# Expert results weighted as they leave PSUM and added to the residual rows in DRAM by an accumulating scatter

## The chip, the cores and the metric

One core of one Trainium2 chip runs the kernel. The metric is the device time of one execution in microseconds (us), lower is better. The timed runs of a kernel carry no profile; one more run is profiled, and every duration of the rows below comes from that one.

## What is computed

A transformer block with two halves. The first half (a hybrid mixer of spatial gating, chunked linear attention and a short convolution) gives the rows `x2 = x + gt1 * mixer`. The second half is a mixture of experts over the 1024 rows: 32 experts in 4 groups, each token goes to the best 2 experts of one group. Then one RMS norm over the sum.

```python
def moe(h, router_w, router_b, w1, w3, w2):
    ...
    weights = top_p / jnp.sum(top_p, axis=-1, keepdims=True)
    ...
    def expert_block(args):
        xb, e = args
        return (jax.nn.silu(xb @ w1[e]) * (xb @ w3[e])) @ w2[e]
    ...
    out = jnp.einsum('nk,nkd->nd', weights.astype(h.dtype), y_assign)
...
        x = x + gt2 * moe(h, router_w, router_b, exp_w1[l], exp_w3[l], exp_w2[l])
    return rmsnorm(x, g_final)
```

T = 1024 rows of D = 1024 float32 values, 512 hidden values in an expert; an expert has three matrices (w1, w3, w2) of 2 MiB each, so 32 experts are 96 units of 2 MiB.

## The kernel before

The program is written by hand for each engine, with semaphores between them; an engine's instructions run in the order of the code. The 1024 rows are 8 tiles of 128. The first 500 us are the mixer. Between about 440 and 530 us the rows x2 are made tile by tile and stored in the DRAM tensor `x2_dram` (a normed copy goes to `xn2_dram`), and the router runs for two tiles at a time: `choose` picks the two experts of each token, `weigh` (from L1685) makes its two shares `top_w`, `place` its position in each expert's list. The matmuls of `listing` (L976) build the lists of rows for each expert, and after the experts have been ranked by their number of rows three small matmuls (L1021 to L1023) give `slot_i`: for each of 25 passes and each of 128 partitions the assignment (2 x token + choice) that the partition holds, or a number past the end where it holds none. `slot_tok` is half of it, the token.

**The expert loop** has 25 passes. Passes 0 to 3 are single: one expert, up to 128 rows. Then come 7 triples of a couple pass (two experts with up to 64 rows each, in the two halves of the partitions) and two single passes; a couple uses 6 units of weights, a single 3. In pass i:

- SP loads the units in the order of `stream` into 9 slots; the load of a unit waits until the unit 9 places before it has been used (`load_unit`, L506).
- POOL gathers the rows of pass i+4 from `xn2_dram` (`gather`, L667) and scatters the result of pass i-1 (`scatter`, L675).
- PE turns the gathered rows (L1030), multiplies by w1 and w3 (L1044 for a single, L1049 for a couple), turns the hidden rows (L1057) and multiplies by w2 (L1068 or L1074) into banks 5 and 6.
- DVE takes the result out of the banks times the gate gt2 (`y_evac`, L1806) into one of two buffers `y_sb`; it may overwrite a buffer when the scatter of two passes before has landed.

The scatter of before writes each row of `y_sb` to row `slot_i` of `y_dram`, which has one row for each assignment (2048 rows). No two writes touch the same row, so scatters may overlap in time; rows without an assignment are past the bound and are dropped.

**The tail.** SP waits for all scatters, then loads `y_dram` (8 MiB) in five pieces of 1, 1, 2, 2 and 2 tiles into `yy` (L567). The residual rows `acc` were loaded before that (L547), once their two slots were free. For each tile DVE adds the first choice times its share (L1894) and the second (L1898); ACT sums the squares (L1327); DVE makes the mean (L1339); POOL raises it to the power -0.5 (L586, where the shared `rsqrt` stands); DVE applies it and the gain (L1888); ACT issues the store of the tile (L1323). A branch for experts whose lists are too long (`most > 0`) follows the loop; it isn't entered with these inputs.

## Time and profile before

| | us |
|---|---|
| median of 3 timed runs | 1165.42 |
| their range | 1164.93 to 1166.04 |
| the profiled execution | 1166.22 |
| its span, first to last instruction | 1164.5 |

The span is shorter than the execution by 1.7 us, which lie around it. The rows of the profile name source lines: L1044 is line 1044 of the kernel before. Busy times of matmul are close to the wall time where PE is the bound. "Landing" of a DMA counts from its issue to the last write. The chain that ended last follows the waits back from the end of the program.

### The profile page before, as it was taken

To read this page: it belongs to the slowest core of one execution; us is meant where nothing else is said; L and a number is where in the kernel's file an instruction comes from. 1 tells how busy PE (TensorE), PEld (TensorE's weight loads), DVE (VectorE), ACT (ScalarE), POOL (GpSimd) and SP (SyncE) were. 2 spreads that over 40 slices of the span, in tenths; PEclk is the share of its full clock that TensorE was granted. 3 is DMA by queue.
4 is the path that set the end of the run, shared out by engine and by line. 5 is a ranking of instruction groups with operands and counts; after the bars stand their busy time and mean duration, and the time that the engine had idled before them with its cause. 6 is when DMAs were issued, how large, how long until landed. Compare 5 with 4: busy or idle time off the path is not lost.

```text
span 1164.5 us, 11977 instructions
## 1 busy us (share of the span) xinstructions
PE 1047.4 (90%) x4616; PEld 611.4 (53%) x4616; DVE 394.7 (34%) x827; ACT 198.7 (17%) x435; POOL 106.8 (9%) x135
## 2 busy tenths in 40 slices
PE   4798999999999999943999999999999999999920
PEld 2487888878896555532444443444444344444410
DVE  2588543426631355551111211211111121121137
ACT  5611125222221121110100100100010010010002
POOL 2000000002100010123010010001001001000013
PEclk9899999999999999955999999999999999999975
DMA  9829311112132662137688999999999999997446
GB/s 370 305 73 343 130 37 37 39 53 91 37 127 91 235 252 92 55 127 261 244 308 329 391 422 387 426 397 405 399 405 416 372 427 385 408 375 302 165 199 243
DMA packets 52555, 295.76 MB, mean 254 GB/s; under 512 B 11129, under 2 KB 23434, under 8 KB 36114
## 3 DMA queue, kind: packets, MB, share of 16 engines
q1 hardware_dynamic: 43634, 274.00, 60.3%
q0 software_dynamic: 7712, 16.80, 3.7%
q10 hardware_dynamic: 1152, 4.19, 0.9%
q8 instruction: 37, 0.61, 0.2%
q14 instruction: 20, 0.16, 0.0%
HBM read 278.55 MB, written 25.85 MB: 261 GB/s over the span
## 4 chain that ended last, share of the span: by engine, by line
PE 87%; DMA 5%; DVE 3%; issue 1%; DVEq 1%; ACT 1%; POOL 1%; SPq 0%; ACTq 0%; POOLq 0%
PE bank L1044 22%; PE bank L1068 11%; PE bank L937 10%; PE bank L1049 8%; PE bank L1074 4%; PE bank L778 3%; PE bank L773 3%; PE bank L775 3%; PE bank L774 3%; PE bank L779 3%; PE bank L780 3%; PE bank L1030 2%; DMA arena<-in_x_dram 1%; PE bank L732 1%; PE bank L955 1%
## 5 line engine op out<-in xcount | busy, mean ns | idle before, releaser
L1044 PE MATMUL bank<-arena 128*128 128x512 f32 x576 | 255.9, 600 | 1.6 <-ACT arena L1295 1.6
L1044 PEld LDWEIGHTS bank<-arena 128*128 128x128 f32 x576 | 109.2, 192 | 145.3 <-issue 143.3
L1068 PE MATMUL bank<-arena 128*128 128x512 f32 x288 | 127.9, 597 | 1.7 <-issue 1.7
L937 PE MATMUL bank<-arena 128*128 128x512 f32 x256 | 114.6, 602 | 0.1
L1049 PE MATMUL bank<-arena 128*64 128x512 f32 x448 | 99.2, 595 | 0.0
L1303 ACT ACTIVATE arena<-bank 128x512 f32<-128x512 f32 x25 | 14.9, 597 | 470.1 <-PE bank L1044 334.2
L778 PE MATMUL bank<-low_r 128*128 128x256 f32 (+1 forms) x320 | 93.7, 293 | 0.0
L779 PE MATMUL bank<-low_r 128*128 128x256 f32 (+1 forms) x320 | 90.8, 284 | 0.0
L780 PE MATMUL bank<-low_r 128*128 128x256 f32 (+1 forms) x320 | 90.8, 284 | 0.0
L1068 PEld LDWEIGHTS bank<-arena 128*128 128x128 f32 x288 | 53.2, 190 | 63.8 <-issue 62.3
L773 PE MATMUL bank<-low_r 128*128 128x512 f32 x192 | 78.1, 407 | 4.9 <-DVE arena L1448 3.7
L1806 DVE TENSOR_TENSOR arena<-bank,arena 128x512 f32<-128x512 f32 x50 | 32.2, 686 | 145.9 <-PE bank L1068 105.3
L937 PEld LDWEIGHTS bank<-arena 128*128 128x128 f32 x256 | 48.1, 192 | 55.8 <-issue 55.8
L774 PE MATMUL bank<-low_r 128*128 128x512 f32 x192 | 76.1, 396 | 0.0
L775 PE MATMUL bank<-low_r 128*128 128x512 f32 x192 | 76.0, 396 | 0.0
L586 POOL TENSOR_TENSOR stats<-stats,half 128x1 f32<-128x1 f32 (+1 forms) x34 | 31.1, 918 | 482.2 <-DVE stats L1339 455.4
L1800 DVE COPY arena<-bank 128x512 f32<-128x512 f32 x25 | 17.3, 692 | 164.2 <-PE bank L1057 164.2
L675 POOL DMA_INDIRECT y_dram<-arena,slot_i x25 | 25.1, 1004 | 506.0 <-DVE arena L1806 506.0
L1049 PEld LDWEIGHTS bank<-arena 128*64 128x64 f32 x448 | 30.9, 137 | 66.6 <-issue 66.6
L1822 DVE TENSOR_TENSOR arena<-bank,arena 128x512 f32<-128x512 f32 x25 | 17.3, 692 | 141.9 <-PE bank L1044 101.7
L778 PEld LDWEIGHTS bank<-low_r 128*128 128x128 f32 x320 | 60.9, 190 | 3.4 <-issue 2.7
L779 PEld LDWEIGHTS bank<-low_r 128*128 128x128 f32 x320 | 61.0, 191 | 0.0
(246 smaller groups left out, 1131.0 us busy)
## 6 DMA issues: line engine op xcount, KB each, us to landing
arena<-in_exp_w_dram SPq DMA_DIRECT2D x96, 2048.0 KB, 11.2
arena<-in_w_ada_dram SPq DMA_DIRECT2D x24, 1024.0 KB, 9.1
low<-in_w_in_dram SPq DMA_DIRECT2D x11, 1024.0 KB, 5.5
arena<-y_dram SPq DMA_DIRECT2D x3, 2048.0 KB, 17.1
arena<-in_x_dram SPq DMA_DIRECT2D x2, 2048.0 KB, 7.8
arena<-in_w_out_dram SPq DMA_DIRECT2D x2, 2048.0 KB, 8.7
arena<-in_x_dram SPq DMA_DIRECT2D x8, 512.0 KB, 3.6
x_dram<-arena SPq DMA_DIRECT2D x8, 512.0 KB, 2.6
```

The costliest lines, as they stand in the source:

```text
L773: pe.matmul(out_[:], hi[:, k, f_], hT_hi[:, k, t_], start=first, stop=False)
L774: pe.matmul(out_[:], lo[:, k, f_], hT_hi[:, k, t_], start=False, stop=False)
L775: mm = pe.matmul(out_[:], hi[:, k, f_], hT_lo[:, k, t_], start=False, stop=last)
L778: pe.matmul(w, hT_hi[:, k, t_], hi[:, k, :], start=first, stop=False)
L779: pe.matmul(w, hT_hi[:, k, t_], lo[:, k, :], start=False, stop=False)
L780: mm = pe.matmul(w, hT_lo[:, k, t_], hi[:, k, :], start=False, stop=last)
L937: mm = pe.matmul(bank[2 * (t % 2) + n][:], yT[:, t, k, :], wout[n][:, k, :], start=(k == 0), stop=(k == KD - 1))
L1044: mm = pe.matmul(out_[:], x[:, k, :], ws[0][:, k, :], start=(k == 0), stop=(k == KD - 1))
L1049: mm = pe.matmul(out_[rows_, :], x[:, k, rows_], w[:, k, :], start=(k == 0), stop=(k == KD - 1))
L1068: mm = pe.matmul(bank[5 + j][:], hT_sb[:, k, :], ws[0][:, k, cols], start=(k == 0), stop=(k == KF - 1))
L1074: mm = pe.matmul(bank[5 + j][rows_, :], hT_sb[:, k, rows_], w[:, k, cols], start=(k == 0), stop=(k == KF - 1))
L1806: ins = TT(y_sb[i % 2][:, j * 512:(j + 1) * 512], bank[5 + j][:], gt2[:, j * 512:(j + 1) * 512], ALU.mult)
```

## The change

- `y_dram` is gone. The rows are scattered into `x2_dram` itself, indexed by the token, with `compute_op=ALU.add`: the DMA reads the old row, adds, and writes.
- The share of each row is applied earlier: `y_evac` multiplies bank, the share `slot_w` of the partition and gt2 in one scalar_tensor_tensor. To have the share by partition, the lists carry a second set of 32 columns: `weigh` writes `named` also with top_w (one drain and two multiplications more), the matmul of `listing` has 64 columns of `named` where it had 32, and three more matmuls pick the shares, after three more DVE instructions (`fits`, `fits`, `share_f`) ahead of `list_f`.
- Every scatter waits until the one before has landed (`scat` is one semaphore now). A couple pass, in which a token may stand twice, is scattered as two transfers of 128 rows, each with the other half's rows past the bound (`half_tok`). That makes 32 scatters of 25.
- In the tail `acc` is loaded after the last scatter, in the same five pieces, at 4 MiB in all, and the early load of 4 MiB is gone. The 16 multiply-adds of L1894 and L1898 are gone; ACT waits for the pieces itself.

The diff, without the branch that isn't entered:

```diff
     xn2_dram = nc.dram_tensor("xn2_dram", (T, D), F32, kind="Internal").ap()
-    y_dram = nc.dram_tensor("y_dram", (2 * T, D), F32, kind="Internal").ap()
+    share_dram = nc.dram_tensor("share_dram", (2 * T, 1), F32, kind="Internal").ap()
     gate_dram = nc.dram_tensor("gate_dram", (2, D), F32, kind="Internal").ap()
...
-        sel, named, r_["t"] = (X.take(4, E) for _ in range(3))
+        sel, named, r_["t"] = X.take(4, E), X.take(4, 2 * E), X.take(4, E)
         M = Region(TMP_AT, TMP_END)
...
         y_sb = [M.take(D) for _ in range(2)]
-        list_f = y_sb[0][0:E, P:2 * P]
+        list_f, share_f = y_sb[0][0:E, P:2 * P], y_sb[0][0:E, 2 * P:3 * P]
+        fits = y_sb[0][0:E, 0:1]
+        slot_w, ov_share = M.take(PASSES), M.take(1)
+        half_tok = M.take(2, COUPLES).bitcast(I32)
         key_row, above = y_sb[1][0:E, 0:E], y_sb[1][0:E, E:2 * E]
...
                          .rearrange("p a n -> p (a n)")).then_inc(S["early_ld"], 16)
-            for s in acc_slots:
-                kind, i, _ = [u for n, u in enumerate(stream) if n % SLOTS == s][-1]
-                sp.wait_ge(S[{"w1": "h1_mm", "w2": "y_mm", "w3": "h3_mm"}[kind]], i + 1)
-            sp.dma_start(acc, x2_dram.rearrange("(t p) d -> p t d", p=P)).then_inc(S["early_ld"], 16)
-
             most = sp.value_load(most_i[0:1, 0:1], min_val=0, max_val=T)
...
-            for h in range(2):
-                sp.wait_ge(scat[h], 16 * ((PASSES + 1 - h) // 2))
+            sp.wait_ge(scat, 16 * added[-1])
             for h, (a, b) in enumerate(y_parts):
-                sp.dma_start(yy[:, a:b, :], y_t[:, a:b, :]).then_inc(y_ld[h], 16)
+                sp.dma_start(acc[:, a:b, :], x2_p[:, a:b, :]).then_inc(y_ld[h], 16)
             sp.wait_ge(out_st, 16 * TILES)
...
                 gp.wait_ge(S["y_ready"], i + 1)
-                gp.sem_inc(S["gp_passed"], 1)
-                gp.indirect_dma_start(out=y_dram, out_offset=bass.IndirectOffsetOnAxis(ap=slot_i[:, c_:c_ + 1], axis=0),
-                                      in_=y_sb[i % 2], in_offset=None, bounds_check=2 * T - 1,
-                                      oob_is_err=False).then_inc(scat[i % 2], 16)
+                for n in range(len(passes[i])):
+                    tok = slot_tok[:, c_:c_ + 1] if len(passes[i]) == 1 else half_tok[:, n, c_ - WIDE:c_ - WIDE + 1]
+                    wait(gp, scat, 16 * (added[i] - len(passes[i]) + n))
+                    gp.sem_inc(S["gp_passed"], 1)
+                    gp.indirect_dma_start(out=x2_dram, out_offset=bass.IndirectOffsetOnAxis(ap=tok, axis=0),
+                                          in_=y_sb[i % 2], in_offset=None, bounds_check=T - 1,
+                                          oob_is_err=False, compute_op=ALU.add).then_inc(scat, 16)
...
                 for n in range(4):
-                    mm = pe.matmul(bank[7][0:E, P:2 * P], named[:, n, :], placed[:, n, :], start=(i == 0 and n == 0),
+                    mm = pe.matmul(bank[7][0:2 * E, P:2 * P], named[:, n, :], placed[:, n, :], start=(i == 0 and n == 0),
                                    stop=(i == TILES // 2 - 1 and n == 3), skip_group_check=True)
...
             pe.wait_ge(S["list_ready"], 1)
-            pe.matmul(bank[7][:, 0:WIDE], list_f, ranked[:, 0:WIDE], start=True, stop=True)
-            pe.matmul(bank[7][0:HALF, WIDE:PASSES], list_f[:, 0:HALF], ranked[:, WIDE:WIDE + COUPLES], start=True, stop=True)
-            pe.matmul(bank[7][HALF:P, WIDE:PASSES], list_f[:, 0:HALF], ranked[:, WIDE + COUPLES:E], start=True,
-                      stop=True).then_inc(S["slots_mm"], 1)
+            for at_, lists in ((0, list_f), (PASSES, share_f)):
+                wide_, couple_ = slice(at_, at_ + WIDE), slice(at_ + WIDE, at_ + PASSES)
+                pe.matmul(bank[7][:, wide_], lists, ranked[:, 0:WIDE], start=True, stop=True)
+                pe.matmul(bank[7][0:HALF, couple_], lists[:, 0:HALF], ranked[:, WIDE:WIDE + COUPLES], start=True, stop=True)
+                mm = pe.matmul(bank[7][HALF:P, couple_], lists[:, 0:HALF], ranked[:, WIDE + COUPLES:E], start=True, stop=True)
+            mm.then_inc(S["slots_mm"], 1)
...
             for t in range(TILES):
-                act.wait_ge(S["fin_acc"], t + 1)
+                for h, (a, b) in enumerate(y_parts):
+                    if a == t:
+                        act.wait_ge(y_ld[h], y_ld_was[h] + 16)
                 act.activation(sq_junk, acc[:, t, :], ACT.Square, accum_out=ssf[:, t:t + 1])
...
                     dve.tensor_reduce(top2[:, :, k], by_tile2(g_["r" if k else "t"]), AX, ALU.add)
-                    TT(named[:, 2 * k:2 * k + 2, :], sel[:, 2 * k:2 * k + 2, :], each(aid_f[:, ts, k], E), ALU.mult)
+                    TT(named[:, 2 * k:2 * k + 2, 0:E], sel[:, 2 * k:2 * k + 2, :], each(aid_f[:, ts, k], E), ALU.mult)
                     TT(r_["t"][:, 2 * k:2 * k + 2, :], sel[:, 2 * k:2 * k + 2, :], eidx.unsqueeze(1).to_broadcast([P, 2, E]), ALU.mult)
...
                 TT(top_w[:, ts, :], top2, each(w_rec, 2), ALU.mult)
+                dve.drain()
+                for k in range(2):
+                    TT(named[:, 2 * k:2 * k + 2, E:], sel[:, 2 * k:2 * k + 2, :], each(top_w[:, ts, k], E), ALU.mult)
...
             dve.wait_ge(S["list_mm"], TILES // 2)
+
+            TS(fits, sort_col[:, 4:5], float(WIDE), float(cap - HALF), ALU.is_lt, ALU.mult)
+            dve.drain()
+            STT(fits, fits, float(HALF), sort_col[:, 2:3], ALU.add, ALU.is_ge)
+            dve.drain()
+            TS(share_f, bank[7][E:2 * E, P:2 * P], fits, None, ALU.mult)
             TS(list_f, bank[7][0:E, P:2 * P], float(NONE), None, ALU.add).then_inc(S["list_ready"], 1)
...
             TS(slot_tok, slot_i, 1, None, ALU.logical_shift_right).then_inc(S["slots_ready"], 1)
+            dve.memset(half_tok.rearrange("p a b -> p (a b)"), 2 * T)
+            dve.drain()
+            for n in range(2):
+                rows_ = slice(n * HALF, (n + 1) * HALF)
+                dve.tensor_copy(half_tok[rows_, n, :], slot_tok[rows_, WIDE:PASSES])
+            dve.tensor_copy(slot_w, bank[7][:, PASSES:2 * PASSES])
+            dve.drain()
...
                 dve.wait_ge(S["y_mm"], i + 1)
-                wait(dve, scat[i % 2], 16 * (i // 2))
+                if i >= 2:
+                    dve.wait_ge(scat, 16 * added[i - 2])
+                c_ = passes[i][0]
                 for j in range(2):
-                    ins = TT(y_sb[i % 2][:, j * 512:(j + 1) * 512], bank[5 + j][:],
-                             gt2[:, j * 512:(j + 1) * 512], ALU.mult)
+                    ins = STT(y_sb[i % 2][:, j * 512:(j + 1) * 512], bank[5 + j][:], slot_w[:, c_:c_ + 1],
+                              gt2[:, j * 512:(j + 1) * 512], ALU.mult, ALU.mult)
                 ins.then_inc(S["y_ready"], 1)
...
-            dve.wait_ge(S["early_ld"], 32)
+            dve.wait_ge(S["early_ld"], 16)
...
             for t in range(TILES):
-                for h, (a, b) in enumerate(y_parts):
-                    if a == t:
-                        dve.wait_ge(y_ld[h], y_ld_was[h] + 16)
-                STT(acc[:, t, :], yy[:, t, 0:D], top_w[:, t, 0:1], acc[:, t, :], ALU.mult, ALU.add)
-                dve.drain()
                 if t:
                     mean_of_tile(t - 1)
-                STT(acc[:, t, :], yy[:, t, D:], top_w[:, t, 1:2], acc[:, t, :], ALU.mult, ALU.add).then_inc(S["fin_acc"], 1)
-                if t:
                     finish(t - 1)
```

The order of the instructions moves at two places.

POOL's queue in the expert loop, from the gather of pass 8 on, first before, then with the change. `y_ready` counts results in `y_sb`, `xt_tr` the turned inputs, `scat` the landed scatters.

```order
L667 DMA arena<-xn2_dram,slot_tok 128x1024 [waits xt_tr]
L675 DMA y_dram<-arena,slot_i 2048x1024 [waits y_ready]
L667 DMA arena<-xn2_dram,slot_tok 128x1024 [waits xt_tr]
L675 DMA y_dram<-arena,slot_i 2048x1024 [waits y_ready]
L667 DMA arena<-xn2_dram,slot_tok 128x1024 [waits xt_tr]
```

With the change:

```order
L666 DMA arena<-xn2_dram,slot_tok 128x1024 [waits xt_tr]
L677 DMA x2_dram<-arena,slot_tok 1024x1024 [waits y_ready,scat]
L666 DMA arena<-xn2_dram,slot_tok 128x1024 [waits xt_tr]
L677 DMA x2_dram<-arena 1024x1024 [waits y_ready,scat]
L677 DMA x2_dram<-arena 1024x1024 [waits scat]
L666 DMA arena<-xn2_dram,slot_tok 128x1024 [waits xt_tr]
L677 DMA x2_dram<-arena,slot_tok 1024x1024 [waits y_ready,scat]
```

A single's scatter gains a wait on the transfer before it; a couple's becomes two, and the gather that follows stands behind the landing of the first of the two. The two rows without `slot_tok` are the two transfers of the couple pass 4.

DVE's queue in the tail, for the first tiles. `fin_ss` is the sum of squares from ACT, `fin_rs` the power from POOL, `wout_ld0`, `wout_ld1` and `y_ld2` the first pieces of the load.

```order
L1894 SCALAR_TENSOR_TENSOR arena<-arena,top_w 128x1024 [waits wout_ld0,early_ld]
L1898 SCALAR_TENSOR_TENSOR arena<-arena,top_w 128x1024
L1894 SCALAR_TENSOR_TENSOR arena<-arena,top_w 128x1024 [waits wout_ld1]
L1339 TENSOR_SCALAR stats<-stats 128x1 [waits fin_ss]
L1898 SCALAR_TENSOR_TENSOR arena<-arena,top_w 128x1024
L1888 SCALAR_TENSOR_TENSOR arena<-arena,stats 128x1024 [waits fin_rs]
L1894 SCALAR_TENSOR_TENSOR arena<-arena,top_w 128x1024 [waits y_ld2]
L1339 TENSOR_SCALAR stats<-stats 128x1 [waits fin_ss]
```

With the change:

```order
L1353 TENSOR_SCALAR stats<-stats 128x1 [waits fin_ss,early_ld]
L1919 SCALAR_TENSOR_TENSOR arena<-arena,stats 128x1024 [waits fin_rs]
L1353 TENSOR_SCALAR stats<-stats 128x1 [waits fin_ss]
L1919 SCALAR_TENSOR_TENSOR arena<-arena,stats 128x1024 [waits fin_rs]
L1353 TENSOR_SCALAR stats<-stats 128x1 [waits fin_ss]
```

The two multiply-adds of each tile are gone, and with them all that DVE did between the mean and the last multiplication.

On ACT the squares of a tile (L1341 with the change) wait for the piece of the load that holds it, where they waited for DVE's second addition; the store of tile t-1 still stands behind the squares of tile t.


## Rows read from the trace of the kernel before

**Rows 1.** Page, part 4: the chain that ended last, shares by engine.
```profile
PE 87%; DMA 5%; DVE 3%; issue 1%; DVEq 1%; ACT 1%; POOL 1%; SPq 0%; ACTq 0%; POOLq 0%
```

**Rows 2.** Busy in stretches: stretch, length, engines, PE clock, DMA share, GB/s.
```profile
739.24:806.70 67.46, 67.37 (x230) 29.48 (x229) 12.12 (x24) 6.31 (x15) 6.10 (x6) 1.00 0.99 406
```

**Rows 3.** Chain in order of time, tail: start, us, what.
```profile
1117.39 3.18 DMA y_dram<-arena,slot_i
...
1121.44 11.46 DMA arena<-y_dram
...
1134.52 1.52 POOL stats L586
...
1138.87 1.52 POOL stats L586
```

**Rows 4.** Timeline of the tail: start, us, engine line op.
```profile
1128.24 1.06 ACT L1327 ACTIVATE arena<-arena 128x1024 f32<-128x1024 f32 x1 [37.13 <-DVE arena L1898]
...
1129.48 0.15 DVE L1339 TENSOR_SCALAR stats<-stats 128x1 f32<-128x1 f32 x1
...
1157.77 1.28 DVE L1888 SCALAR_TENSOR_TENSOR arena<-arena,stats 128x1024 f32<-128x1024 f32 x1 [0.43 <-POOL stats L586]
...
1158.97 0.15 DVE L1339 TENSOR_SCALAR stats<-stats 128x1 f32<-128x1 f32 x1
1159.09 2.34 ACTq L1323 DMA_DIRECT2D out_dram<-arena  x2
1159.20 0.54 POOL L586 TENSOR_TENSOR stats<-stats,half 128x1 f32<-128x1 f32 x1 [1.46 <-DVE stats L1339]
1159.78 1.28 DVE L1888 SCALAR_TENSOR_TENSOR arena<-arena,stats 128x1024 f32<-128x1024 f32 x1 [0.65 <-POOL stats L586]
```

**Rows 5.** Page, part 6: DMA issues, count, KB each, median us to landing.
```profile
arena<-in_x_dram SPq DMA_DIRECT2D x8, 512.0 KB, 3.6
x_dram<-arena SPq DMA_DIRECT2D x8, 512.0 KB, 2.6
```

**Rows 6.** Landing of scatters L675 in 640:1030, then of all gathers L667.
```profile
DMA to landing us min/median/max: 10.0/10.9/11.8
...
DMA to landing us min/median/max: 5.6/15.5/19.4
```

**Rows 7.** Load of one unit: issue, its landing (us), and its first use.
```profile
970.85 0.33 SPq L506 DMA_DIRECT2D arena<-in_exp_w_dram  x1
...
arena<-in_exp_w_dram SPq DMA_DIRECT2D x1, 2048.0 KB, 11.2
...
1009.08 13.93 PE bank L1044 x32
```

**Rows 8.** DMA packets in 672:740, of all queues, then of POOL's (q0).
```profile
DMA packets 2607, 27.74 MB, mean 408 GB/s; under 512 B 487, under 2 KB 487, under 8 KB 1056
...
q0 software_dynamic: 864, 2.33, 8.6%
```

**Rows 9.** Timeline before the expert loop.
```profile
523.19 0.35 DVE L1708 TENSOR_TENSOR arena<-arena,bank 128x64 f32<-128x64 f32 x2 [0.53 <-PE bank L969]
...
527.81 0.59 PE L1021 MATMUL bank<-ranked,arena 32*128 32x18 f32 x2
...
528.46 0.25 PE L1023 MATMUL bank<-ranked,arena 32*64 32x7 f32 x1
...
529.25 0.18 DVE L1787 TENSOR_SCALAR slot_tok<-slot_i 128x25 int32<-128x25 int32 x1
...
530.39 0.97 POOL L644 DMA_INDIRECT list_dram<-aid,idx_now  x1 [0.30 <-issue]
531.66 1.04 POOL L667 DMA_INDIRECT arena<-xn_dram,slot_tok  x1 [0.30 <-issue]
```

**Rows 10.** Groups of DVE instructions by form: count, busy, mean ns, idle before.
```profile
L1806 DVE TENSOR_TENSOR arena<-bank,arena 128x512 f32<-128x512 f32 x50 | 32.2, 686 | 145.9 <-PE bank L1068 105.3 <-PE bank L1074 40.7
...
L1518 DVE SCALAR_TENSOR_TENSOR arena<-bank,arena 128x512 f32<-128x512 f32 x8 | 5.1, 684 | 0.5 <-PE bank L775 0.5
```

40 lines of the change are left out of this document (24 added, 16 removed).

## The prediction

> **What bounds the kernel now.** I read the chain that ended last first. PE holds 87% of it [rows 1], and in the expert loop a period of three passes (one couple, two singles) takes 67.46 us with PE busy for 67.37 of them at the full clock [rows 2]. So in the loop only what makes PE wait counts. The same row shows the DMA engines at 99% busy with 406 GB/s: there is little room for more traffic. Then I read the tail, from the last scatter on. PE has nothing to do there, so every microsecond counts. The last scatter lands 3.18 us after 1117.39, at 1120.57; the load of y_dram follows, and then a chain of VectorE and GpSimd with one tile each 4.35 us (from one power at 1134.52 to the next at 1138.87) [rows 3]. From the landing to the end of the span (1164.5) are 43.9 us.
>
> **The tail, which the change shortens.** A tile now needs its square sum, mean, power, last multiplication. From the rows of before: a square's start to the mean's is 1.24 us (1128.24 to 1129.48) [rows 4]. The last tile shows mean, power and multiplication with nothing beside them, as all tiles will have it: mean at 1158.97, power at 1159.20 with 0.54 us, multiplication at 1159.78, done at 1161.06, so 2.09 us. The power in mid-tail takes 1.52 us [rows 3] since it starts while L1898 runs; with that gone I take 0.54. The next mean starts 1.20 us after the start of the multiplication before it (1157.77 to 1158.97) [rows 4], so the period is 0.81 + 1.20 = 2.01 us instead of 4.35. ACT stays under it: the square of tile t+1 stands behind the store issue of tile t-1, whose multiplication ends 2.09 us after its mean; with 0.4 us for the issue (two issues end at 1161.43) and 1.24 for the square that is 3.73 us from mean t-1 to mean t+1, under the 4.02 of two periods.
>
> The first piece is 512 KiB instead of 1 MiB; loads of that size land 3.6 us after issue [rows 5]. All 4 MiB: the third piece of before ended the first 4 MiB at 1132.90, 12.3 us after the scatter's landing [rows 3]. The last two tiles are wanted for their squares at 3.7 + 1.24 + 6 x 2.01 - 1.24 = 15.8 us. By then about two stores of 512 KiB have been in the way (2.6 us at most), which leaves about 1 us of cover; if it is gone, each us shows in full.
>
> Sum from the last landing to the end: 3.6 + 0.1 (wake) + 1.24 + 7 x 2.01 + 2.09 + 3.4 (from 1161.06 to 1164.5, the last store) = 24.5 us against 43.9. **Gain 19.4 us.** If the stores and loads collide I allow 3 us less.
>
> **The last scatter, which the change lengthens.** The trace has no accumulating DMA. It moves the same rows and reads the old ones as well, which excludes a gain; the floor is 3.18 us, so +0. The far row is a whole gather ahead of the write: the fastest gather lands in 5.6 us [rows 6], so +5.6. A load of 512 KiB takes 1.0 us more than a store of it (3.6 and 2.6) [rows 5]; this is the nearest, as a scatter waits for a read's way and no more if rows overlap. I take +1.5. What was issued early for `acc` is gone and gives nothing back: nothing waited for it.
>
> **Ahead of the loop.** The drain and two multiplications in `weigh` cost some 0.45 us on VectorE. For the last pair of tiles they fall into the 0.53 us in which L1708 waits for PE [rows 9]; for the others the router's work lies beside the output projection. The three new small instructions and the three matmuls move `slot_tok`: three instructions and drains of some 0.25 us as its own row has them, and matmuls of 0.90 us like L1021 to L1023 (527.81 to 528.71). From 529.43 it goes to about 531.1. The first gather starts at 531.66 and comes behind four list scatters of GpSimd, the last at 530.39 with 0.97 us [rows 9]: hidden, by a little. I book +0.1, and 0 to +0.8 as bounds. `half_tok` and `slot_w` come while VectorE waits for the first gather.
>
> **In the loop.** The scalar_tensor_tensor form in `y_evac` costs the same as the old one (684 ns in L1518 with a bank as input, 686 in L1806) [rows 10]. The new wait is GpSimd's: the next scatter, and behind it in the queue the gather of four passes later, wait for the scatter before. A scatter under full weight traffic lands after 10.9 us, at most 11.8 [rows 6]; a period of three passes now holds four of them in series. VectorE may overwrite a buffer when the scatter of two passes before has landed, and there PE would stand behind it. In series they fit as long as 4 x (L + 0.2) < 67.46, so **L < 16.7 us**. Under that the loop is unchanged; above it each further microsecond costs 4 us in each of about 5.5 periods (the last couple meets no weight traffic any more), less some 5 us that the two buffers give at the start, so 22 x (L - 16.7) - 5: L = 18 gives about +24, L = 20 about +68.
>
> How large is L? 864 packets in 68 us for three scatters and three gathers [rows 8] are 144 each: nine for each of 16 engines (eight rows and a completion). A scatter has 10.9 - 3.2 = 7.7 us more than an undisturbed one, so 0.86 us for each packet that takes its turn among the weights' packets. Low end: no turn more, L = 10.9. High end: each packet takes two turns, L = 10.9 + 7.7 = 18.6. But of the 2607 packets of that stretch 487 are under 512 B: rows past the bound and completions. Of the 8 rows of an engine about 4 are real, so two turns for those give +3.4, L = 14.3. I take 13, and book 0 us.
>
> **The traffic.** The old rows are read: in each period four experts' scatters of about 1.2 MB (half of the 2.33 MB of GpSimd's queue in rows 8), which at 406 GB/s is 2.9 us if the engines had no room at all. In 6.5 periods that is 19 us by which the weights could fall behind. A unit issued at 970.85 lands 11.2 us later, at 982.0, and is first used at 1009.08, 27 us later [rows 7]; it is the least cover I found in any period, and it doesn't shrink from one to the next. 19 is under 27: 0 us.
>
> A page of the Trainium skill speaks against the change here. "Collectives: The Full Stack", section "The bandwidth ceiling: the fold count and why AG ≠ RS ≠ AR", says that an adding transfer needs two source reads on the same ring and so runs at about half the rate of a copy. No row of before shows it; by that rule the scatters' share would double, which is the 19 us just worked out, and the result stays.
>
> **Sum.** -19.4 + 1.5 + 0.1 = -17.8 us. Against the profiled execution of 1166.2 that is 1148.4; the median of the timed runs lies 0.8 lower, so 1147.6. I say **1148**.
>
> **Rivals.**
> 1. *The scatters in series become the bound of the loop* (slower). For it: four instead of three in a period, in the one stretch where the engines are 99% busy. Against: it needs L over 16.7, 54% above the median row. It decides where the time lost passes the gain of 17.8: at L = 17.7. With two turns for every packet, L = 18.6, the loop loses about 37 us, and the kernel takes 1148 + 37 = 1185; were L twice the row (21.8) it would be 1255. GpSimd would show scatters back to back, and PE waits at L1068. 19%.
> 2. *One engine finishes an adding row before it starts the next packet, whosever it is* (weights late). Each real row then blocks 16 engines for a read and a write instead of a copy. 2048 rows are 128 for each engine; the cover of 27 us is used up at 0.2 us a row, and the gain at 0.35. From there on slower; with 0.5 us a row the loop loses 37 us, 1185. For it: nothing in the trace. "DMA: Bandwidth & Descriptors", section "Two DMAs through the same engine are not ordered", of the Trainium skill tells of read-modify-write packets where the second reads before the first has written, so they overlap; no row here shows it, and I keep the chance at 5%.
> 3. *L just over the bound, or the weights late by a little*: the loop loses 1 to 15 us, 1149 to 1163. 7%.
> 4. *The tail gives little*, as loads and stores hold each other up or the scatter's reads are slow: 1155. Its time lies in the range; 6%.
>
> My forecast itself has 63%, with its own range from 1145 (no cost of the last scatter, full gain) to 1154 (+5.6, +0.8).
>
> **Chances and range.** A measurement tells 0.2% from no change, 2.3 us. Faster than 1163.1: 63 + 6 + 7 = 76%. Slower than 1167.8: of 24% for rivals 1 and 2 a little lies between, so 22%. The same: 2%. The range: from 1144 up over cases 3 and 4 (76%) and into rival 1 as far as L = 18.1 (+26 us), 1144 to 1173, where L = 18.1 is nearly two turns for every packet.
>
> **What would show it.** Landing of scatters in the loop under 16.7 us, and no wait of VectorE for them. PE's period 67.46 us. First use of weights still over 10 us after landing. The last scatter's landing under 5 us. Power at 0.54 us and multiplications each 2.0 us in the tail. Wrong it would be if PE waits in the loop, if the power stays at 1.5 us, or if the squares wait for pieces of the load.

## The result and the profile after

| | before | with the change |
|---|---|---|
| median | 1165.39 us (4 runs) | **1151.82 us** (4 runs) |
| range | 1164.93 to 1166.04 | 1151.10 to 1153.15 |
| profiled execution | 1166.2 | 1151.10 |
| its span | 1164.5 | 1149.3 |

The ratio is 0.9884 (95% interval 0.9867 to 0.9902): faster by 13.6 us where the forecast of 1148 meant 17.4. The same kernel run once more gave 1151.5 us and 0.9885 (a_again, below). PE still holds the chain, and a period of the loop has the same length and the same PE time as in [rows 2].

Page, part 4, and busy in stretches (columns as in [rows 2]), of the changed kernel:

```profile
PE 88%; DMA 5%; DVE 3%; ACT 1%; issue 1%; DVEq 1%; SPq 0%; POOL 0%; ACTq 0%; POOLq 0%
...
739.24:806.70 67.46, 67.37 (x229) 29.50 (x228) 12.48 (x25) 6.31 (x15) 9.43 (x7) 1.00 1.00 398
```

Apart from 1 us at the start of the loop (last section but two), loss and gain therefore lie at the end. The chain in order of time, the counterpart of [rows 3]:

```profile
1116.42 6.28 DMA x_dram<-arena,slot_tok
...
1124.56 15.16 DMA arena<-x_dram
...
1139.74 1.06 ACT arena L1341
```

The last scatter takes 6.28 us (3.18 in [rows 3]) and lands at 1122.70. From there to the end are 26.6 us (43.9 before). Timeline of the tail (start, us, engine line op, in brackets the idle time before and what ended it), the counterpart of [rows 4]:

```profile
1127.98 1.29 DVE L1919 SCALAR_TENSOR_TENSOR arena<-arena,stats 128x1024 f32<-128x1024 f32 x1 [0.68 <-POOL stats L585]
...
1129.98 1.28 DVE L1919 SCALAR_TENSOR_TENSOR arena<-arena,stats 128x1024 f32<-128x1024 f32 x1 [0.65 <-POOL stats L585]
1131.11 1.06 ACT L1341 ACTIVATE arena<-arena 128x1024 f32<-128x1024 f32 x1 [2.79 <-DMA arena<-x_dram]
...
1133.12 1.28 DVE L1919 SCALAR_TENSOR_TENSOR arena<-arena,stats 128x1024 f32<-128x1024 f32 x1 [0.65 <-POOL stats L585]
...
1139.13 1.28 DVE L1919 SCALAR_TENSOR_TENSOR arena<-arena,stats 128x1024 f32<-128x1024 f32 x1 [0.65 <-POOL stats L585]
1139.74 1.06 ACT L1341 ACTIVATE arena<-arena 128x1024 f32<-128x1024 f32 x1 [1.77 <-DMA arena<-x_dram]
...
1141.18 0.54 POOL L585 TENSOR_TENSOR stats<-stats,half 128x1 f32<-128x1 f32 x1 [2.09 <-DVE stats L1353]
...
1141.75 1.28 DVE L1919 SCALAR_TENSOR_TENSOR arena<-arena,stats 128x1024 f32<-128x1024 f32 x1 [0.65 <-POOL stats L585]
...
1143.76 1.28 DVE L1919 SCALAR_TENSOR_TENSOR arena<-arena,stats 128x1024 f32<-128x1024 f32 x1 [0.65 <-POOL stats L585]
```

Multiplications start every 2.00 us, except twice: 3.14 us to tile 2 and 2.62 us to tile 6, behind squares that waited for a piece of the load.

In the loop three things moved without touching PE. The landing of the scatters in 640:1030 (all from L677, counterpart of [rows 6]), the wait of POOL for the scatter before in the whole loop, and the queues in 672:740 (counterpart of [rows 8]):

```profile
DMA to landing us min/median/max: 9.8/12.6/13.5
...
  DMA x_dram<-arena: 75.8, 8
...
q0 software_dynamic: 1008, 2.33, 13.5%
```

And the load of the same unit as in [rows 7]: issue, landing in us, first use.

```profile
969.74 0.33 SPq L508 DMA_DIRECT2D arena<-in_exp_w_dram  x1
...
arena<-in_exp_w_dram SPq DMA_DIRECT2D x1, 2048.0 KB, 26.0
...
1007.97 13.93 PE bank L1056 x32
```

It lands at 995.7, 12.2 us before its use, where [rows 7] had 27.

### The profile page after: what moved, and what is told of

It is laid out like the page before. It is cut to its first block, busy times and chain, and to the rows that moved or that the text cites. A ratio compares the mean times of both kernels' runs of the same rounds, so it can differ in the third digit from the quotient of the medians.

```text
span 1149.3 us, 12006 instructions
## 1 busy us (share of the span) xinstructions
PE 1047.8 (91%) x4622; PEld 612.6 (53%) x4622; DVE 380.5 (33%) x826; ACT 198.7 (17%) x435; POOL 125.5 (11%) x142
## 4 chain that ended last, share of the span: by engine, by line
PE 88%; DMA 5%; DVE 3%; ACT 1%; issue 1%; DVEq 1%; SPq 0%; POOL 0%; ACTq 0%; POOLq 0%
PE bank L1056 22%; PE bank L1080 11%; PE bank L947 10%; PE bank L1061 9%; PE bank L1086 4%; PE bank L788 4%; PE bank L783 3%; PE bank L785 3%; PE bank L784 3%; PE bank L789 3%; PE bank L790 3%; PE bank L1042 2%; DMA arena<-in_x_dram 1%; PE bank L742 1%; DMA arena<-x_dram 1%; PE bank L965 1%
## 5 line engine op out<-in xcount | busy, mean ns | idle before, releaser
L1838 DVE SCALAR_TENSOR_TENSOR arena<-bank,arena 128x512 f32<-128x512 f32 x50 | 35.2, 746 | 146.0 <-PE bank L1080 105.3
L585 POOL TENSOR_TENSOR stats<-stats,half 128x1 f32<-128x1 f32 (+1 forms) x34 | 24.3, 716 | 475.0 <-DVE stats L1353 448.1
L1830 DVE COPY arena<-bank 128x512 f32<-128x512 f32 x25 | 17.3, 692 | 164.2 <-PE bank L1069 164.2
L1854 DVE TENSOR_TENSOR arena<-bank,arena 128x512 f32<-128x512 f32 x25 | 17.3, 692 | 139.0 <-PE bank L1056 99.6
L788 PEld LDWEIGHTS bank<-low_r 128*128 128x128 f32 x320 | 60.9, 190 | 3.4 <-issue 2.7
L789 PEld LDWEIGHTS bank<-low_r 128*128 128x128 f32 x320 | 61.0, 191 | 0.0
L790 PEld LDWEIGHTS bank<-low_r 128*128 128x128 f32 x320 | 61.0, 190 | 0.0
```

The lines of the kernel that those rows point to most:

```text
L788: pe.matmul(w, hT_hi[:, k, t_], hi[:, k, :], start=first, stop=False)
L789: pe.matmul(w, hT_hi[:, k, t_], lo[:, k, :], start=False, stop=False)
L790: mm = pe.matmul(w, hT_lo[:, k, t_], hi[:, k, :], start=False, stop=last)
L1838: ins = STT(y_sb[i % 2][:, j * 512:(j + 1) * 512], bank[5 + j][:], slot_w[:, c_:c_ + 1], gt2[:, j * 512:(j + 1) * 512], ALU.mult, ALU.mult)
```

## The experiments

Ratios are to the kernel before, run beside each of them; the number in brackets is their 95% interval.

**e1_plain: the change without the addition.** The scatters overwrite rows, so the sum of the residual and the two results is left out.

```diff
                                           in_=y_sb[i % 2], in_offset=None, bounds_check=T - 1,
-                                          oob_is_err=False, compute_op=ALU.add).then_inc(scat, 16)
+                                          oob_is_err=False).then_inc(scat, 16)
```

> The changed kernel with a plain write in place of the adding one (the result of the experts overwrites the residual rows, so the sum is left out); the series of one transfer at a time, the 32 transfers and the tail stay. Theory (adding costs reads that the loop hides and a longer last transfer): loop landings fall from 12.8 to about 10.9 us, POOL's time for one scatter from 1.55 to 1.0 us, the last landing from 6.3 to about 3.2, the cover of the weights stays at 27 us through the loop, and the time falls by the 3.1 us of the last transfer, to about 1148.7. Rival (the last transfer is longer for its place in the tensor or its indices, not for the adding): landing stays near 6 us and the time at 1151.8.

Measured 1149.3 us (1148.1 to 1150.72), ratio 0.9875 [0.9853, 0.9898]. Of e1: the scatter's own time on POOL (min/median/max ns), its landings in 640:1030, the queue in 672:740, the last scatter.

```profile
L677 POOL DMA_INDIRECT x_dram<-arena,slot_tok x18: 962/998/1018, 584.7 to 1117.5; - x18
...
DMA to landing us min/median/max: 7.3/10.7/11.3
...
q0 software_dynamic: 1008, 2.33, 9.3%
...
1117.51 0.96 POOL L677 DMA_INDIRECT x_dram<-arena,slot_tok  x1 [15.37 <-DVE arena L1838]
```

Those scatters land like the old ones, and the last one lands after 3.2 us. With the same 1008 packets POOL's queue takes 9.3% instead of 13.5%: the addition alone is 4.2% of a 67.5 us period, 2.8 us, and no part of it is the larger number of packets. The cover of the weights is back too. The unit of [rows 7] is issued at 970.83 in e1 and first used at 1008.99, 27 us after its landing, where the changed kernel has 12:

```profile
arena<-in_exp_w_dram SPq DMA_DIRECT2D x1, 2048.0 KB, 11.5
```

The timed runs don't show the expected 3.1 us: by the ratios e1 is 1.0 us below the changed kernel, with overlapping intervals, and its median is near the expected 1148.7 in part because the kernel before, too, was faster beside it (1163.99). In the profiles, by the spans (1147.2 and 1149.3), it is 2.1 us: 3.1 us less for the last scatter, and a loop that ended 1.1 us later (the scatter starts at 1117.51, not 1116.42). The tail from the last landing takes 26.5 us here too, so reading rows just added to isn't what makes it long.

**e3_series_only: the kernel before, each scatter waiting for the one before.**

```diff
                 gp.wait_ge(S["y_ready"], i + 1)
+                if i:
+                    gp.wait_ge(scat[(i - 1) % 2], 16 * ((i + 1) // 2))
                 gp.sem_inc(S["gp_passed"], 1)
```

> The kernel before with the wait alone: a scatter is issued when the one before has landed (25 transfers, plain). Theory: three transfers of 10.9 us in a period of 67.5 us, no engine waits for them: 1165.4, within 0.5 us. Rival (POOL's queue stands behind the wait, and the gathers come late): PE waits at its turns, over 1168.

Measured 1164.68 us, ratio 1.0001 [0.9989, 1.0012]. The series by itself is free, for three plain transfers a period.

**e2_add_only and e2b_add_only: the kernel before, adding into y_dram.** y_dram is filled with x first, so the output has x in it besides. e2b places the fill behind two other units of w_in.

```diff
+                        sp.dma_start(y_dram[h * T:(h + 1) * T, :], x[0]).then_inc(y_ld[4], 16)
...
-                                      oob_is_err=False).then_inc(scat[i % 2], 16)
+                                      oob_is_err=False, compute_op=ALU.add).then_inc(scat[i % 2], 16)
...
+            gp.wait_ge(y_ld[4], 32)
```

> The kernel before with the adding form alone: scatters add into y_dram, whose rows are filled with x beforehand (so the sum starts from x, not from nothing), they overlap as before and are 25. Theory: the loop is unchanged, the last transfer lands after about 6.3 us instead of 3.2, cover of the weights shrinks by about 2.5 us a period; 1165.4 + 3.1 = 1168.5. Rival (the adding form itself slows PE's loop when transfers overlap, and only the series hides it): more than 1172.

Measured 1181.1 us, ratio 1.0153 [1.0128, 1.0177], a miss, by a fault of the experiment: the fill stood in the way of a unit of w_in, and the mixer waited. The chain of e2:

```profile
294.75 22.84 DMA low<-in_w_in_dram
```

> As e2_add_only (the kernel before with the adding form alone, transfers overlapping, y_dram filled with x beforehand), with the filling moved to where it delays no load of the first half. Theory: the 11 us that e2_add_only lost ahead of the loop are gone, and what stays is the last transfer: 3 us over the kernel before. Rival (the adding costs PE time in the loop when transfers overlap): over 8 us.

Measured 1167.73 us, ratio 1.0021 [1.0011, 1.0031], 2.5 us over before. Last scatter in the chain of e2b, and landings in 640:1030:

```profile
1115.38 6.21 DMA y_dram<-arena,slot_i
...
DMA to landing us min/median/max: 12.4/12.8/13.3
```

The addition has the same price in another destination and without the series: +3.0 us for the last scatter, +1.9 us under weight traffic, and nothing in the loop (PE is busy for 389.44 of the 390 us of 640:1030, 389.46 before). Since e1 and e2b each isolate it, the price is shown, not argued.

**e4_six: six transfers in series in a period instead of four.** From pass 4 on singles are split in two halves as well.

```diff
-        added = [sum(len(p) for p in passes[:i + 1]) for i in range(PASSES)]
+        parts = [2 if i >= 4 else 1 for i in range(PASSES)]
+        added = [sum(parts[:i + 1]) for i in range(PASSES)]
...
-                for n in range(len(passes[i])):
+                for n in range(parts[i]):
```

> The changed kernel with the single passes from 4 on also scattered as two transfers, so six in series in each period of 67.5 us instead of four; same rows, same result. Theory (the series is free only while its sum is under the period): each landing 10 to 12.4 us and 0.86 us to the next issue make 68 to 79 us, over the period: VectorE waits for a free buffer and PE behind it, and the time rises by 16 us (at 11.3 us a transfer) to 50 us, to 1168 to 1200, with the last transfers late by some 8 to 14 us more. Rival (half the rows make a half transfer take half the time): each landing 7 us, six of them 47 us, and the time stays at 1152.

Measured 1170.01 us, ratio 1.0059 [1.0037, 1.0081], 20 us over the changed kernel by the ratios. Of e4: who DVE's evacuation waits for (us, times), a stretch of the loop, and the landings of its scatters in 640:1030.

```profile
  DMA x_dram<-arena: 194.5, 12
...
874.00:940.00 66.00, 62.18 (x192) 27.84 (x191) 10.15 (x20) 4.69 (x11) 12.29 (x9) 0.95 0.96 373
...
DMA to landing us min/median/max: 7.7/12.4/13.6
```

A transfer with half of its rows past the bound costs as much time in the series as a full one: 12.4 us here, where nearly all are such halves, and in the changed kernel 12.3 for the halves of couples and 12.9 for singles. Once six of them don't fit in a period DVE waits and PE with it (62.18 of 66.00 busy, at a clock of 0.95). So there is a threshold, somewhere between four and six transfers, and the change stays below it. Where it lies was not measured, and the cost above it is far under the theory, which said 50 us for landings of 12.4. From the first scatter of pass 4 (674.19) to that of pass 19 (1057.69) the series took 383.5 us, 46 more than five periods of 67.46; but the last result left the banks only 19 us later than in the changed kernel (1133.13 and 1114.15). By these figures (an estimate) the series can fall some 27 us behind before PE has to follow.

**e7_traffic: six copies of 2 MiB from DRAM to DRAM more in the loop,** one in each of six periods.

```diff
+                if n % 12 == 8 and 20 <= n < 92:
+                    sp.dma_start(spare[more], w1_v[more]).then_inc(S["more_ld"], 16)
```

> The changed kernel with a copy of 2 MiB from DRAM to DRAM more in each of six periods of the expert loop, on SP's queue, of no use to the result. Theory (the reads of the adding scatters are paid from the cover of the weights, which fell from 27 to 10.6 us): six copies of 2 MiB at 400 GB/s are 31 us, more than the cover that is left, so PE waits for weights late in the loop and the time rises by about 20 us, to 1172. Rival (the engines still had room, the cover is not what pays): less than 3 us.

Measured 1172.71 us, ratio 1.0078 [1.0049, 1.0106]. Waits of PE in e7:

```profile
PE bank L1092 <- DMA arena<-in_exp_w_dram: 8.2, 3, 3.5
PE bank L1067 <- DMA arena<-in_exp_w_dram: 8.1, 4, 2.9
```

That is 21 us over a_again, as the theory said (31 us of copies less 10.6 of cover, about 20), and 22 by the ratios. The cover that the change leaves can be used up, and beyond it traffic costs time directly. The changed kernel still has 12 us of cover for the unit shown above, so its own distance to the bound is about that.

**a_again: the changed kernel once more, beside e5 and e7.**

> The changed kernel once more, beside the others of this job, for comparisons of a microsecond: 1151.8, within 1.5. In its profile the stretch at which the granted clock of PE rises to full at the start of the expert loop (553 to 556 us) may lie some 2 us earlier or later than in the profile before, which is worth about 1 us of the span either way.

Measured 1151.5 us (1150.41 to 1152.11), ratio 0.9885 [0.9868, 0.9901]: last scatter 5.91 us, last piece 16.9 us after its landing, the end 26.5 us after it.

Why do the pieces land late? Two causes were open: the stores of finished tiles meet the loads, or the rows are shorter. The kernel before reads 8 KiB of y_dram for a token, the changed one 4 KiB of x2_dram. The next four runs separate them.

**e5_sp_stores: SP gives out the stores, behind the loads.**

```diff
+            for t in range(TILES):
+                sp.wait_ge(S["fin_out"], t + 1)
+                sp.dma_start(out_t[t], acc[:, t, :]).then_inc(out_st, 16)
```

> The changed kernel with the stores of the result issued from SP, behind the five loads in SP's own queue, instead of from ACT. Theory (in the tail the stores of ACT's queue take turns with the loads, so the pieces of the load come late and the squares wait for them): the last piece lands 12.3 us after the last scatter instead of 17.0, no square waits for a piece of it, a multiplication starts every 2.0 us to the end, and the time falls by 1.5 to 2 us against a_again. Rival (the pieces come late by themselves, with rows of 4 KiB where the kernel before had 8): the last piece still lands at about 17 us and the time stays.

Measured 1152.27 us, ratio 0.9892 [0.9876, 0.9909]: no gain. The last piece came 14.8 us after the scatter's landing instead of 17.0, but the third was as late as ever (8.7 us after the scatter, 8.4 in the changed kernel), and the tail took 26.4 us where it had 26.6.

**e5_held: ACT gives out all stores after the last square.**

```diff
-                if t:
-                    store(t - 1)
-            store(TILES - 1)
+            for t in range(TILES):
+                store(t)
```

> The changed kernel with all eight stores after the last square on ACT, so that no store meets a load at all, with the 4 KiB rows of the changed kernel. It shows how fast the pieces come alone. Theory A of e6: the third and the last piece are still late (last landing 14 to 15 us after the scatter's, GB/s about 350 to 360), so the square of tile 2 still waits for it. Theory B: the last piece lands 12.3 us after the scatter as in the kernel before, and no square waits. In both the time is worse than the changed kernel's, by 3 to 7 us, since the last squares end about 14 us before the end and 4 MiB of stores take about 12 us from then on, with one issue of 0.1 us to 0.5 us each: about 1152 to 1156.

Measured 1153.51 us, ratio 0.9899 [0.9882, 0.9915]. With no store beside the loads the last piece landed at 1137.3, 13.7 us after the scatter, between the 14 to 15 of theory A and the 12.3 of B, nearer to A; the third landed after 8.6 us, and the square of tile 2 still waited 2.84 us for it.

**e6_rows: a partition's tokens are neighbours in memory,** rows of 8 KiB in the pieces of two tiles.

```diff
-        x2_p = x2_dram.rearrange("(t p) d -> p t d", p=P)
+        x2_p = x2_dram.rearrange("(p t) d -> p t d", p=P)
...
-        out_t = out[0].rearrange("(t p) d -> t p d", p=P)
+        out_t = out[0].rearrange("(p t) d -> t p d", p=P)
```

> The tail of the changed kernel again, but a partition's eight tokens are neighbours in memory (token = 8p + t instead of 128t + p), so that a piece of two tiles moves as rows of 8 KiB where it moved as two rows of 4 KiB; the stores stay at 4 KiB. It tells the length of the rows from the collision of loads and stores. In the changed kernel the last piece landed 17.0 us after the last scatter's landing where 12.3 were expected, and multiplications were late by 1.1 and 0.6 us at tiles 2 and 6. Theory A (the 4 KiB rows make the pieces slow by themselves): the DMA engines move about 425 GB/s in the first five microseconds of the loads instead of 350 to 360, the last piece lands within 14 to 15 us, both late multiplications are gone, and the time falls by 1.5 to 2 us, to about 1150. Theory B (only the stores are in the way): nothing moves, 1151.5 to 1152.

Measured 1150.72 us (1149.09 to 1152.35), ratio 0.9877 [0.986, 0.9893]. The late multiplication of tile 6 is gone, that of tile 2 is 0.4 us late instead of 1.1; the last piece landed 15.3 us after the scatter, the end came 25.8 us after it. Part of the gain is lost at the start: the first piece (one tile, still in rows of 4 KiB, now 32 KiB apart) lands after 3.7 us instead of 3.1, and the first multiplication starts 0.6 us later.

**e8_rows_sp: e6 and e5 together.**

> Neighbouring tokens for a partition as in e6, and the stores given out by SyncE behind the loads as in e5. In e5 the last piece came 2 us earlier, and nothing was gained, since the third piece was still late. By theory A of e6 both causes are away here: the last piece lands 12.5 to 13.5 us after the last scatter, no square waits after the first, and the time is 1149 to 1150, 1.5 to 2.5 us below the changed kernel. By theory B of e6 it is 1152 as e5 was.

Measured 1150.92 us (1148.56 to 1152.38), ratio 0.9878 [0.9859, 0.9897]. The last piece landed 13.0 us after the scatter, all multiplications start every 2.0 us, the end comes 25.3 us after the landing. The five microseconds from 3 us after the last scatter's landing on, in before, changed kernel, e5_held, e6_rows and e8_rows_sp (last columns: DMA share, GB/s):

```profile
1123.57:1128.57 5.00, 0.00 (x0) 0.00 (x0) 2.93 (x3) 0.33 (x1) 0.00 (x0) 0.50 1.01 424
```
```profile
1125.70:1130.70 5.00, 0.00 (x0) 0.00 (x0) 2.22 (x4) 2.30 (x4) 1.10 (x2) 0.50 0.98 367
```
```profile
1126.65:1131.65 5.00, 0.00 (x0) 0.00 (x0) 2.09 (x4) 2.30 (x4) 1.10 (x2) 0.50 0.98 377
```
```profile
1126.30:1131.30 5.00, 0.00 (x0) 0.00 (x0) 1.65 (x4) 2.30 (x4) 1.10 (x2) 0.50 1.02 417
```
```profile
1125.94:1130.94 5.00, 0.00 (x0) 0.00 (x0) 1.81 (x4) 2.96 (x5) 1.10 (x2) 0.50 1.02 428
```

The same stretch of eight more profiles agrees. Seven with rows of 4 KiB (changed kernel, a_again, e1, e4, e7, e5_sp_stores, e5_held) move 338 to 384 GB/s at a DMA share of 0.93 to 0.99, store or no store; six with 8 KiB (before, e2b, e3, e6, e8, e9) move 417 to 431 at 1.00 to 1.03. e6 also changed how far the rows lie apart, but the kernel before, whose rows of 8 KiB follow each other, has the same rate.

By the pieces: the third lands 8.4 to 8.7 us after the scatter in all seven with 4 KiB, wherever the stores are given out, after 8.2 in e6 and after 7.3 in e8. The last lands after 17.0 us, 14.8 with the stores behind the loads, 13.7 with none beside them, 15.3 with the longer rows and 13.0 with both. So moving the stores does nothing for the third piece unless the rows are longer too, and the last is late through both rows and stores. The profiled tails show this; in the timed medians the gain of e6 and e8 over the changed kernel, about 1 us, is inside the intervals.

**e9_mean_ahead: e8 with the mean of tile t+1 ahead of the multiplication of tile t.**

```diff
+            mean_of_tile(0)
             for t in range(TILES):
-                if t:
-                    mean_of_tile(t - 1)
-                    finish(t - 1)
-            mean_of_tile(TILES - 1)
-            finish(TILES - 1)
+                if t + 1 < TILES:
+                    mean_of_tile(t + 1)
+                finish(t)
```

> e8 (neighbouring tokens for a partition, stores from SyncE) with the mean of tile t+1 taken before the multiplication of tile t instead of behind it, so that GpSimd's power of the next tile runs beside the multiplication. It tells what the power costs when it is covered. In the kernel before the same pair stood side by side: a mean at 1134.29, VectorE's addition from 1134.36, the power 1134.52 with 1.51 us, the next VectorE instruction 0.04 us after the power's end at 1136.07. Theory A (GpSimd's small instruction can't finish while VectorE's long one runs, as in those rows): power 1.5 us, multiplications every 1.71 us instead of 2.01; the first comes 0.7 us later, since it stands behind the mean of tile 1; the end comes 23.9 us after the last scatter's landing instead of 25.2, and the time is 1149.5, about 1.3 below e8. Theory B (the two run side by side undisturbed): power 0.54 us, multiplications every 1.45 us, gain 3.2 us, 1147.7.

Measured 1149.1 us (1146.54 to 1151.75), ratio 0.9852 [0.9832, 0.9872], the best version; the end comes 23.5 us after the last landing (theory A: 23.9). Its interval touches that of the changed kernel (from 0.9867), so that it beats that one is likely, not shown beyond doubt; its gain over e8 is inside the intervals as well. Timeline of e9:

```profile
1133.83 1.28 DVE L1915 SCALAR_TENSOR_TENSOR arena<-arena,stats 128x1024 f32<-128x1024 f32 x1
1133.99 2.02 POOL L588 TENSOR_TENSOR stats<-stats,half 128x1 f32<-128x1 f32 x2 [0.97 <-DVE stats L1349]
...
1135.02 0.15 DVE L1349 TENSOR_SCALAR stats<-stats 128x1 f32<-128x1 f32 x1
...
1135.54 1.29 DVE L1915 SCALAR_TENSOR_TENSOR arena<-arena,stats 128x1024 f32<-128x1024 f32 x1 [0.37 <-POOL stats L588]
...
1136.80 1.28 DVE L1915 SCALAR_TENSOR_TENSOR arena<-arena,stats 128x1024 f32<-128x1024 f32 x1
```

Theory A holds for every other tile: a power that starts 0.16 us after the multiplication took 1.5 us. The next power had its mean ready (1135.02) and ran directly behind it; the two together are 2.02 us, so it took some 0.5 us although the next multiplication started at 1135.54. The distances are 1.71 and 1.26 us in turn, neither theory's.

## Why the prediction was right, and where it was not

The forecast of 1148 (own range 1145 to 1154) had the sign, the place and the mechanism; it was 3.8 us too low. The stated range of 1144 to 1173 was wide, 29 us, and hitting it says little. (Two slips in it change nothing: 16.7 is 53% above 10.9, not 54%, and 1148 + 26 is 1174.) Two of the signs that the prediction named did not come out: the last scatter landed after 6.28 us where it said under 5, and two squares waited for pieces of the load, which it had listed among what would show it wrong. The other signs held: landings of 12.6 us in the loop with no wait of VectorE for them, a period of 67.46 us, 12 us of cover, power of 0.54 us and multiplications 2.0 us apart. By its steps, on the profiled executions (spans 1164.5 and 1149.3, so 15.2 us of gain where the sum said 17.8):

| step | predicted | measured |
|---|---|---|
| tail from the last landing | 24.5 | 26.6 |
| last scatter | +1.5 | +3.1 |
| ahead of the loop | +0.1 | 0 |
| banks to buffers, last pass | 0 | +0.1 |
| loop | 0 | 0 |
| start of the loop, not part of the change | - | -1.0 |

The sum of the measured column is -17.3 + 3.1 + 0.1 - 1.0 = -15.1.

**Tail.** The frame of it held: power 0.54 us, multiplications every 2.00 us for a predicted 2.01, and the first of them 5.28 us after the landing, 0.5 earlier than in the sum. The term that failed is the load: "4 MiB by 12.3 us, with about 1 us of cover". It was read from pieces with 8 KiB a row, and it allowed for stores but not for shorter rows. The last piece landed 17.0 us after the scatter, and the third was late already, though the first store was issued only at 1129.30. Cost: 1.14 + 0.62 = 1.75 us. e5_held, with no store beside the loads, has the wait at tile 2 as well.

The rest lies behind the last multiplication: from its end to the end of the span it is 4.3 us where 3.4 were taken for "the last store". The last store itself is as fast as before, 2.6 us. What is longer is the end of the program on POOL, whose closing drain ends last, at 1164.2 before and at 1148.8 now, 1.1 us after the last store has landed (the closing instructions are put down to L112; before, then the changed kernel):

```profile
L112 POOLq DRAIN  x1: 5071/5071/5071, 1159.2 to 1159.2; - x1
```
```profile
L112 POOLq DRAIN  x1: 5631/5631/5631, 1143.1 to 1143.1; - x1
```

From the last multiplication to the end it is 3.4 us in the three profiles with 25 scatters (before, e3, e2b), 4.3 in those with 32 (the changed kernel, a_again, e1, e7, e5_sp_stores, e6, e8) and 5.0 in e4 with 46. In e5_held and e9 the last landing of a store sets the end (6.9 and 4.7 us). So in these profiles it goes with the number of scatters, and by e1 it isn't the addition; what POOL does in that time stays open.

-0.5 + 1.75 + 0.85 = +2.1 us. The prediction allowed "3 us less" for collisions of loads and stores. The sum is inside that, in part by luck: 0.85 us of it is no such collision, and of the 1.14 us at tile 2 the stores are not the cause.

**Last scatter.** The value taken, +1.5, was the difference between a load and a store; the true one is 3.1 us (2.7 to 3.1 over the runs), within the bounds 0 to 5.6. 0.6 us of it is POOL's own time, which the prediction did not count at all:

```profile
L677 POOL DMA_INDIRECT x_dram<-arena,slot_tok x18: 1548/1564/1600, 583.6 to 1116.4; - x18
```

The old scatter took 1014 ns there, e1's 998. If that counts in full, the other 2.5 us lie in the transfer; that all 3.1 come with the addition is shown by e1 and e2b.

**Loop, series.** L was predicted 13 us, measured 12.6 in the median and 13.5 at most. The model of one more turn for each real row gave 14.3 us, 3.4 over a plain scatter; the measured 1.7 to 1.9 are half of that. The 13 was picked below the model's value without a reason given, and nothing here shows the turns themselves, so that it came so near is luck. The gap between a landing and the next issue was put at 0.2 us; it is 0.83 us, as POOL's way to the last scatter shows, from the released wait (L676) to the start of the transfer at 1116.42 (chain in order of time; POOLq is POOL's sequencer):

```profile
1115.59 0.04 POOLq L676
1115.63 0.06 issue
1115.70 0.03 POOLq L677
1115.73 0.47 issue
1116.20 0.22 POOLq L691
```

So the bound for four transfers that fit in a period is L < 16.0, not 16.7. It changed nothing, and rival 1 is excluded by L. Its prices were too high: e4 shows that a bound exists, but 9.2 us too much in each period would by the prediction's formula (5.5 periods, less 5 us) cost 46 us, and 19 were measured. The 5 us that it gave the buffers are nearer to 27.

**Loop, traffic.** 2.9 us a period was predicted, e1 against the changed kernel gives 2.8, and the cover fell from 27 us to 12 for the unit of [rows 7], where the sum of 19 us would have left 8. e7 shows what comes behind it. "Collectives: The Full Stack", section "The bandwidth ceiling: the fold count and why AG ≠ RS ≠ AR", of the Trainium skill, which gives the adding step of a collective half the rate of a copy, says nothing of a scatter inside one core; carried over to it, the rule is borne out in direction and nearly in size: if of e1's 9.3% three of seven parts are the gathers (3 gathers and 4 scatters of 144 packets each, an estimate), the scatters' part rose from 5.3% to 9.5%, 1.8 times. Rival 2 (a row that blocks an engine) would at its prices have kept PE waiting; PE is busy for 67.37 of 67.46 us.

**Ahead of the loop.** `slot_tok` came at 531.04 (531.1 predicted) and the first gather at 532.24 instead of 531.66:

```profile
531.04 0.18 DVE L1810 TENSOR_SCALAR slot_tok<-slot_i 128x25 int32<-128x25 int32 x1
...
532.24 1.04 POOL L666 DMA_INDIRECT arena<-xn_dram,slot_tok  x1 [0.30 <-issue]
```

The 0.6 us are not the added instructions. The last matmuls of the router were already as much later (chain in order of time, before and with the change), and the gather follows them by 8.9 us in both:

```profile
522.73 0.44 PE bank L969 x2
```
```profile
523.32 0.44 PE bank L979 x2
```

From there `slot_tok` comes 7.72 us later instead of 6.52, so the added instructions cost 1.2 us for the 1.65 of the prediction, all of it hidden; that its time of 531.1 was met is luck. What comes ahead of the loop differs from one execution to the next: in the profiles with the added instructions `slot_tok` lies between 531.0 and 533.4. In this pair the first gather landed at the same time, 545.6.

**Evacuation.** The form with the share as a scalar is not free but 60 ns dearer (686 ns in [rows 10]), which shows only in the last pass, twice:

```profile
L1838 DVE SCALAR_TENSOR_TENSOR arena<-bank,arena 128x512 f32<-128x512 f32 x50 | 35.2, 746 | 146.0 <-PE bank L1080 105.3
```

**The 1.0 us at the loop's start** is PE's clock, which in this execution was full from 553 on where that of before reached it later. The same stretch in the changed kernel, in before and in a_again (second to last columns: granted clock, DMA share, GB/s):

```profile
553.00:556.00 3.00, 3.00 (x9) 1.33 (x8) 0.00 (x0) 0.00 (x0) 0.00 (x0) 1.00 0.30 122
```
```profile
553.00:556.00 3.00, 3.00 (x6) 1.20 (x5) 0.00 (x0) 0.00 (x0) 0.00 (x0) 0.64 0.36 145
```
```profile
553.00:556.00 3.00, 3.00 (x7) 1.39 (x6) 0.00 (x0) 0.00 (x0) 0.00 (x0) 0.77 0.73 294
```

In a_again, the same kernel, it is between the two. From the first matmul of the loop to the last scatter it is 571.7 us in before and 570.7 in the changed kernel, but 571.4 in e3 and 570.5 in e2b, whose loop starts as that of before. So it isn't an effect of the change, and the profile alone makes the gain 1 us larger than it is. What sets the moment stays open.

## What to carry to other kernels

Work that a DMA can do while TensorE is the bound (here the combination of expert results) is worth moving out of a tail where nothing covers it; the price is paid at the end alone (3.1 us of the last transfer, and here 0.9 us of a longer end of the program), as long as the series of dependent transfers fits between the uses of its buffers and the weights keep some of their cover. Work out both limits first: six transfers instead of four, or 2 MiB more for each period, turned the gain of 14 us into a loss of 7 to 9 by the ratios. Past a limit, count the slack that the buffers give before charging the excess in full. When a load is costed from another row of the profile, compare the length of its contiguous rows and not only the bytes.

## What the runs showed of the hardware

- An accumulating indirect scatter of 128 rows of 4 KiB lands after 5.9 to 6.3 us undisturbed, a plain one after 3.2; under full weight traffic 12.6 to 12.8 against 10.7 to 10.9. POOL is busy for 1.56 us with it instead of 1.0.
- One with half of its rows past the bound saves nothing noticeable in a series under traffic: 12.4 us in e4, and 12.3 against 12.9 for full ones in the changed kernel.
- Between the landing of one scatter and the issue of the next that waits for it POOL lets 0.83 us pass (1141.49 to 1142.32 in e4).
- With the DMA engines 93 to 100% busy, loads in rows of 4 KiB moved 338 to 384 GB/s and in rows of 8 KiB 417 to 431.
- From the last multiplication to the end of the span it took 3.4, 4.3 and 5.0 us with 25, 32 and 46 scatters in the program, plain or adding; why is open.
- A small GpSimd operation that starts beside a long VectorE scalar_tensor_tensor lasts until 0.4 us after that has ended (1.5 us for 0.54), as in [rows 3] and e9; one that starts just ahead of it does not (0.5 us, e9).
